# A two-layer transformer, a chunked attention with an RWKV recurrence and a mixture of experts on one core: spreading column values with matmuls instead of transposes

## The reference

```python
def rms_norm(x, g):                       # over the whole token, over one head of 64, or over 128 values
    y = x * lax.rsqrt(jnp.mean(x * x, axis=-1, keepdims=True) + EPS)
    return y * g
...
qa = apply_rope(rms_norm(qa.reshape(bsz, length, H_A, D_A), g_qa), cos, sin)
ka = apply_rope(rms_norm(ka, g_ka), cos, sin)                       # one key head
qb = apply_rope(rms_norm(qb.reshape(bsz, length, H_B, 2, D_B), g_qb), cos, sin)
kb = apply_rope(rms_norm(kb.reshape(bsz, length, H_B, 2, D_B), g_kb), cos, sin)
...
o_b = rms_norm(o_b, g_subln) * (1.0 - lam_init)                     # the attention's sub-norm
...
kk = kk * lax.rsqrt(jnp.maximum(jnp.sum(kk * kk, axis=-1, keepdims=True), 1e-24))   # per head of 64
...
yn = ((y - m) * lax.rsqrt(var + GN_EPS)).reshape(B, S, D_RWKV)      # group norm, per head of 64
```

## Time and profile before

| | |
|---|---|
| median of 3 runs | 2809.46 us (2809.1 to 2816.86) |
| the profiled execution | 2809.1 us, its span 2807.6 us |
| mean granted PE clock | 0.979 |
| PE busy | 2642.6 us, 94% of the span, 14834 records |
| DVE busy | 1647.5 us, 59% |
| ACT busy | 1189.3 us, 42% |
| POOL busy | 138.7 us, 5% |

### The profile page before, as it was taken

The page is one execution under the profiler, slowest core; times in us unless marked ns, Lnnn a source line. Parts: engine busy times, 40 slices in busy tenths (PEclk is TensorE's granted clock), DMA queues, the critical chain, the costliest instruction groups (busy, mean ns, idle before and its releaser), DMA issues.

```text
span 2807.6 us, 36515 instructions
## 1 busy us (share of the span) xinstructions
PE 2642.6 (94%) x14834; PEld 1992.0 (71%) x14834; DVE 1647.5 (59%) x2744; ACT 1189.3 (42%) x1815; POOL 138.7 (5%) x101
## 2 busy tenths in 40 slices
PE   6999999999999999999999999999999989989878
PEld 4777677888876786767888887676776758745446
DVE  4698556645446488655645455445435534489767
ACT  3226543423334224653424234345322324388765
POOL 0020000000000020000000000000000000033210
PEclk9999999999999999999999999999999989999999
DMA  3112232232221222233223222312111124599982
GB/s 139 61 64 102 72 124 98 90 104 91 92 89 64 77 74 81 85 109 109 90 90 105 90 91 90 120 55 78 58 49 42 35 95 142 205 382 396 401 335 97
DMA packets 64144, 334.95 MB, mean 119 GB/s; under 512 B 9570, under 2 KB 10338, under 8 KB 31076
## 3 DMA queue, kind: packets, MB, share of 16 engines
q1 hardware_dynamic: 58852, 324.15, 32.0%
q0 software_dynamic: 5120, 8.40, 0.9%
HBM read 312.59 MB, written 28.31 MB: 121 GB/s over the span
## 4 chain that ended last, share of the span: by engine, by line
PE 84%; DVE 7%; ACT 5%; issue 3%; DMA 1%; SPq 0%; POOLq 0%; DVEq 0%; ACTq 0%
PE bank L911 15%; PE bank L913 15%; PE bank L912 15%; PE bank L1091 4%; PE bank L1093 3%; PE bank L1092 3%; PE bank L3212 2%; PE bank L3213 2%; PE bank L3228 2%; PE bank L2310 2%; PE bank L1135 2%; PE bank L1165 1%; PE bank L1155 1%; PE bank L1082 1%; PE bank L2297 1%
## 5 line engine op out<-in xcount | busy, mean ns | idle before, releaser
L911 PE MATMUL bank<-XH,wh 128*128 128x512 f32 x1328 | 530.5, 399 | 13.2 <-DVE XL L1387 8.9
L913 PE MATMUL bank<-XH,wl 128*128 128x512 f32 x1328 | 519.6, 391 | 0.0
L912 PE MATMUL bank<-XL,wh 128*128 128x512 f32 x1328 | 519.5, 391 | 0.0
L1346 DVE TENSOR_TENSOR wl<-raw,wh 128x2048 fp32r<-128x2048 f32 (+1 forms) x165 | 364.0, 2208 | 155.6 <-ACT wh L1878 155.6
L1878 ACT ACTIVATE wh<-raw 128x2048 fp32r<-128x2048 f32 (+1 forms) x165 | 303.4, 1840 | 178.7 <-DMA raw<-in_W 178.6
L911 PEld LDWEIGHTS bank<-XH,wh 128*128 128x128 f32 x1328 | 249.8, 188 | 87.9 <-DVE XL L1387 18.2
L912 PEld LDWEIGHTS bank<-XL,wh 128*128 128x128 f32 x1328 | 250.3, 188 | 53.4 <-issue 3.2
L913 PEld LDWEIGHTS bank<-XH,wl 128*128 128x128 f32 x1328 | 249.9, 188 | 53.9
L911 PE MATMUL bank<-arena_rounded,wh 128*128 128x512 f32 x576 | 230.6, 400 | 5.3 <-DVE arena_rounded L1592 3.2
L912 PE MATMUL bank<-arena_rounded,wh 128*128 128x512 f32 x576 | 229.1, 398 | 0.0
L913 PE MATMUL bank<-arena_rounded,wl 128*128 128x512 f32 x576 | 229.0, 398 | 0.0
(11 more groups left out here) (541 smaller groups left out, 4478.8 us busy)
## 6 DMA issues: line engine op xcount, KB each, us to landing
raw<-in_W SPq DMA_DIRECT2D x153, 1024.0 KB, 4.9
arena<-in_WE SPq DMA_DIRECT2D x40, 1024.0 KB, 25.6
wh_full<-in_WE SPq DMA_DIRECT2D x19, 1024.0 KB, 26.9
raw<-in_WE SPq DMA_DIRECT2D x18, 1024.0 KB, 26.4
gsave<-scr SPq DMA_DIRECT2D x48, 256.0 KB, 2.2
scr<-gsave SPq DMA_DIRECT2D x48, 256.0 KB, 3.8
hT<-in_WE SPq DMA_DIRECT2D x12, 1024.0 KB, 26.3
cst<-in_WE SPq DMA_DIRECT2D x7, 1024.0 KB, 26.9
```

The costliest lines, as they stand in the source:

```text
L911: pe.matmul(ps[0:c.stop - c.start, :], h[:, k, c], hi, start=i == 0, stop=False)
L912: pe.matmul(ps[0:c.stop - c.start, :], h[:, k, c], lo, start=False, stop=False)
L913: mm = pe.matmul(ps[0:c.stop - c.start, :], l[:, k, c], hi, start=False, stop=i == len(xs) - 1)
L1346: w_lo.inc(dve.tensor_tensor(wl[:, i % 3, 0:k], raw[:, i % 3, 0:k], wh[:, i % 3, 0:k].bitcast(F32), ALU.subtract), i)
```

## The change

Three edits. `spread` calls a matmul with the identity as the moving operand in place of the transpose, on the same operands. `spread_heads` takes the eight columns themselves and makes two matmuls per 128 tokens, each with a column broadcast to 128x64 as its weights and 64 partitions of the bank as its result; the vector engine's writing out of the columns (for `kkspread` and `gspread`) is dropped. For the keys of RoPE the columns of a whole group are transposed once (`hrt`, at steps 5 and 13, in bank 5, 2 or 8 result rows), the scalar engine copies them to SBUF, and each key pair's factor is one matmul of the constants `hbr` (2 or 8 rows, 128 columns) with these rows. The scalar engine's five copies a layer and their semaphore go.

```diff
@@ plan_win
+                if s in (5, 13):
+                    bank.plan(("hrt", li, s // 4 - 1), 5)
@@ spread
-                    mm = pe.transpose(ps[:, tt(ti)], cols[:, ti:ti + 1].to_broadcast([128, 128]), ident)
+                    mm = pe.matmul(ps[:, tt(ti)], cols[:, ti:ti + 1].to_broadcast([128, 128]), ident, start=True, stop=True)
@@ spread_heads(key, cols, ready, warm=0)
-                    mm = pe.transpose(ps[:, tt(ti)], rows[:, tt(ti)], ident)
+                    for h in range(2):
+                        mm = pe.matmul(ps[64 * h:64 * h + 64, tt(ti)], cols[:, ti, h:h + 1].to_broadcast([128, 64]), ident,
+                                       start=True, stop=True)
@@ tensor engine, first_projections
+                    if s in (5, 13):
+                        gi = s // 4 - 1
+                        n = 2 if gi == 0 else 8
+                        ps = opened(("hrt", li, gi))
+                        pe.wait_ge(*hrec((li, gi)))
+                        for ti in range(4):
+                            mm = pe.transpose(ps[0:n, tt(ti)], rr(li, gi)[:, 8 * ti:8 * ti + n], ident)
+                        bank.filled(mm, ("hrt", li, gi))
...
-                            spread_heads(("hbr", li, t), RT[t % 2], factor((li, t)))
+                            gi, j = t // 4, 0 if t == 3 else t % 4
+                            n = 2 if gi == 0 else 8
+                            ps = opened(("hbr", li, t))
+                            pe.wait_ge(*bank.empty(("hrt", li, gi)))
+                            if t == 3 and li == 0:
+                                pe.wait_ge(c_in, 16)
+                            a, _ = cparts["hbr"]
+                            mm = pe.matmul(ps, cst[0:n, a + 128 * j:a + 128 * j + 128], RT[gi % 2][0:n, :], start=True, stop=True)
+                            bank.filled(mm, ("hbr", li, t))
@@ scalar engine, first_projections (behind the square of the step's pair, ahead of the second relu)
-                    t = rope_at(s)
-                    if t is not None and is_key(t):
-                        gi, j = t // 4, 0 if t == 3 else t % 4
-                        act.wait_ge(*hrec((li, gi)))
-                        if t >= 10:
-                            act.wait_ge(*bank.full(("hbr", li, t - 2)))
-                        cols = rr(li, gi).rearrange("p (t h) -> p t h", t=4)[:, :, 2 * j:2 * j + 2]
-                        factor.inc(act.activation(RT[t % 2].rearrange("p (t h d) -> p t h d", t=4, h=2),
-                                                  bc(cols.unsqueeze(3), [128, 4, 2, 64]), ACT.Copy), (li, t))
+                    if s in (5, 13):
+                        gi = s // 4 - 1
+                        n = 2 if gi == 0 else 8
+                        key = ("hrt", li, gi)
+                        act.wait_ge(*bank.full(key))
+                        bank.emptied(act.activation(RT[gi % 2][0:n, :], bank.ap(key)[0:n, :], ACT.Copy), key)
@@ tensor engine, recurrence
-                spread_heads(("kkspread", j), KSQ, pv(("krec", j)), 3 if j else 2)
+                spread_heads(("kkspread", j), p.kcols.rearrange("p (t h) -> p t h", t=4), pv(("krec", j)), 3 if j else 2)
...
-                spread_heads(("gspread", j), GSQ, sv(("grec", j)))
+                spread_heads(("gspread", j), p.gcols.rearrange("p (t h) -> p t h", t=4), sv(("grec", j)))
@@ vector engine, recurrence (the same for gcols, GSQ and grec)
-                v.inc(dve.reciprocal(p.kcols, p.kcols))
-                dve.wait_ge(*v())
-                pv.inc(dve.tensor_copy(KSQ.rearrange("p (x d) -> p x d", x=8), bc(p.kcols.unsqueeze(2), [128, 8, 64])), ("krec", j))
+                pv.inc(dve.reciprocal(p.kcols, p.kcols), ("krec", j))
```

More of the change, by code:

```diff
@@ L588, in program @@
         turned = Signal(sem("turned"), [(li, t) for li in layers for t in range(16) if not is_key(t)])
-        factor = Signal(sem("factor"), [(li, t) for li in layers for t in range(16) if is_key(t)])
         scored = Signal(sem("scored"), [(li, i) for li in layers for i in range(12)])
@@ L957, in spread, with spread_heads @@
                 for ti in range(4):
-                    mm = pe.transpose(ps[:, tt(ti)], cols[:, ti:ti + 1].to_broadcast([128, 128]), ident)
+                    mm = pe.matmul(ps[:, tt(ti)], cols[:, ti:ti + 1].to_broadcast([128, 128]), ident, start=True, stop=True)
                 bank.filled(mm, key)
-            def spread_heads(key, rows, ready, warm=0):
+            def spread_heads(key, cols, ready, warm=0):
                 ps = opened(key)
@@ L2754, in scan @@
                 dve.wait_ge(*sa(("groot", j)))
-                v.inc(dve.reciprocal(p.gcols, p.gcols))
-                dve.wait_ge(*v())
-                sv.inc(dve.tensor_copy(GSQ.rearrange("p (x d) -> p x d", x=8), bc(p.gcols.unsqueeze(2), [128, 8, 64])), ("grec", j))
+                sv.inc(dve.reciprocal(p.gcols, p.gcols), ("grec", j))
                 yield
```

## The result

The changed kernel took 2830.15 us (median of 4 runs, 2827.71 to 2834.76), the kernel before 2811.28 (4 runs). The ratio is 1.0073, 95% interval 1.0052 to 1.0092: slower by 15 to 26 us, 20.5 by the ratio. The prediction was 2812, with a range to 2822. The record has nine executions of the changed kernel: eight lie between 2827.65 and 2837.99 (their mean is 1.0072 times that of the kernel before, the two medians stand at 1.0067), and the ninth, at a mean granted clock of 0.69, took 3555.43 and is left out.

The account below looks back on a forecast made before the run. The prediction took the PE as the bound (busy 94% of the span, 84% of the chain). Terms 4.1 + 1.8 + 3.9 + 0.2 = +10.0 us and -7 for the clock, on 2809.1, gave 2812, range 2800 to 2822.

Parts of the forecast that it names:

- The price of a burst: Spreads as f32 matmuls: +0.45 us on the PE per burst, +0.9 for the first norm at half clock.
- the overlap of the two halves: Head spreads' 16 records on alternating partition halves run concurrently, 1.09 us; without overlap 1.76.
- the copy of 0.6 on two partitions: RoPE's keys: each new small ACT copy of 512 columns takes 0.6 us.
- step 5: RoPE's keys: the new ACT copy ahead of the second relu delays the next scores, +1.38 us a layer.
- step 6: RoPE's keys: without the factor's copy the relu and rotation start earlier, -0.52 us a layer.
- the recurrence: kkspread and gspread without the vector engine's copy: earlier start offsets longer PE bursts, +0.2 us in all.
- steps 13 to 16: RoPE's keys: PE gains 2.1 us, partly absorbed by the idle of 3.07; attention starts +1.1 us later a layer.
- The clock: Low-clock stretches behind PE idles, 16 us at stake, would partly go: -7 us.
- three stage ends: Recurrence: low-clock stretches, one of 3.4 us worth 1.7 and two of 10.2 worth some 3.7 each.
- the low stretches only move: Rival, whole kernel: the terms stand and the clock gives nothing, 2819 us; chance 0.22.
- the sub-norm's first bursts are free: Attention's sub-norm: first two bursts of each layer covered by four waits of 6.7 us; uncovered 1.8.
- The third possibility of the prediction: Rival: the 1.2 us idle at step 5 brings a low-clock stretch in each layer, 2822 us; chance 0.08.

Follow-up runs that it names:

- b_heads: Kernel before with only the recurrence's two head spreads (kkspread, gspread) as matmuls, without the vector engine's copy: 2812.12 us, 1.0012.
- e_twice: Kernel before with every one-column spread's four transposes made twice, no matmul in it: 2821.9 us, 1.0043.
- f_factor: Kernel before with the scalar engine's factor copy of step 6 moved behind the second relu: 2811.36 us, 1.0009.
- n_norms: Kernel before with the one-column spreads as matmuls in the norms alone, the sub-norm's left as transposes: 2819.43 us, 1.0033.
- s_subs: Kernel before with the one-column spreads as matmuls in the sub-norm alone: 2815.99 us, 1.0021.
- a_spread: Kernel before with only the one-column spreads (norms and sub-norm) as matmuls: 2821.65 us, 1.0042.
- c_keys: Kernel before with only RoPE's key factors made the new way: 2821.49 us, 1.0037.
- d_keys_late: c_keys with the scalar engine's new copy behind the second relu of the step: 2821.77 us, 1.0055 to the kernel before.
- r_subs: s_subs profiled once more with nothing edited: span 2832.8 us.

## Why the prediction was wrong, step by step

**Right.** The price of a burst (some 0.45 on the PE, 0.97 for the first norm, 1.09 for the head spread), the overlap of the two halves, the copy of 0.6 on two partitions, step 5 (1.2 measured, 1.38 forecast), step 6 (0.52), and the recurrence, as far as it can be told: `b_heads` costs nothing that stands clear of its interval. The first two mechanisms of steps 13 to 16 came as described: the vector engine's wait for GpSimd grew from 0.46 to 0.73, with two new waits of 0.34 and 0.30 in front of it, 0.91 together where 0.8 was forecast.

**Mis-sized: steps 13 to 16.** The term was +1.1 a layer; the timeline shows 2.5. Of the difference of 1.4, 0.96 is the vector engine's addition beside GpSimd's second product. The prediction followed GpSimd as something that the vector engine waits for, and not as something that slows it. With it, the keys are 1.2 - 0.5 + 2.5 = 3.2 a layer, 6.4 in place of 3.9, and the sum of the rows is 12.5 in place of 10.0.

**Failed: "The clock", -7.** This is the step that put the result outside. Its reason was that low stretches follow waits, that some of these shrink, and that the spreads among these waits are denser as matmuls. Some waits did shrink, as said above, but the stretches did not go with them: their sum rose from 122 to 142 us in the first pair of profiles and fell from 135 to 130 in the second, and behind the cut of 1696.73 it rose in both, from 91 to 105 and from 91 to 103. Measured +20.5 less 12.5 leaves about +8 (2 to 13 by the interval), of the same size as the term and of the other sign. The prediction also counted three stage ends in its 16 us at stake, where the kernel before has four: one of 3.4 us and three of 10.2, the last at 2308.4. Two pairs of profiles tell where it stands. A cut of the vector engine just ahead of the second model's first projection starts at 1696.73 and 1698.72 in the two profiles of before, and at 1713.84 and 1709.33 in the two of after: the second pair is 10.6 apart, which is about the sum of the rows up to there (6.4 for the keys, 1.8 for the sub-norm, 0.96 + 4 x 0.46 for five norms: 11.0). The first pair is 17.1 apart. The early stretches scatter: ahead of the cut there are 31 and 44 us of low clock in the two profiles of before, 38 and 27 in those of after, so the agreement of the second pair with the sum is in part chance. Behind that point the spans grow by another 9.5 and 7.4, where rows explain 1.4 (three norms). So in these pairs 6.0 to 8.1 us are the late stretches', of which the 12 to 14 us more of low clock account for some 4 to 5 by the slopes above: 1.6 at the entry of the second model and 2.6 of the 3.1 at the first stage end, which the second stage end about gives back (3.4 us of low clock where before had 10.2); the rest lies in others that were not taken apart. The mean granted clock shows less of it than the places do: it was 0.9752 over the changed kernel's four runs and 0.9774 over 65 of the kernel before, worth some 3 us by the last point of this document.

The prediction had put "the low stretches only move" among its rivals at 0.22, with a price of nothing. What it missed is that moving has a price. In the kernel before, some of them lie where the PE is not the limit (the vector engine 3.31 of 3.41 us busy at 195.5, 6.47 of 6.82 at 1062.5, 3.40 of 3.40 at 1714.5). A stretch that leaves such a place gives back little. The first of these shows it: `e_twice`, `b_heads`, `f_factor` and `n_norms` have no low stretch there, yet their vector engine takes the same 50.77 us to the first softmax, and the PE, 1.36 us early, waits for it; its second scores start 0.45 behind the softmax where they started 0.55 behind it. The prediction had taken the full 1.7 us of this stretch as gain. One that lands where the others wait for the PE costs 1.6.

**Still open.** Why the stretch at the first stage end is 3.4 us in some kernels, 10.2 or 13.7 in others and missing in `s_subs` wasn't settled; the unedited part behind the cut shows what they cost, not what sets them. For `a_spread` and `n_norms`, which edit three norms there, that the surplus is the clock's is argued and not shown: from the cut to the end they take 1116.7 and 1119.2 us, with 98 and 107 of low clock, but the mean clock of `a_spread` over its six executions (0.9775) is that of the kernel before. Nor is it shown that the sub-norm's first bursts are free: the four waits of 6.7 us that should have shrunk by 1.8 are 6.2 in `s_subs`, but also 5.3 in `n_norms`, which left the sub-norm alone. The third possibility of the prediction, a low stretch brought about by the wait at step 5, is half supported: every profile with the new step 5 has one that starts between 80 and 93 us, no other has, and most of these lack the one at 107 (`c_keys` has both). It came even in `d_keys_late`, where the wait is gone, so it isn't the wait that brings it.

## What to carry to other kernels

When the PE carries 84% of the chain and the granted clock drops in places, cost an edit by its rows, and treat the clock as a term that can go against you by as much as it can help: here 7 us were counted as its gain and some 8 us were lost, more than most of the edits cost. Keep a part of the program that the edit leaves alone and compare it between profiles: what it gains or loses is not the edit's own work. Look at which engine is full in each low stretch before counting on its removal: one in which the others wait for another engine was worth next to nothing here. Where a second engine shares work with the vector engine, follow what starts beside what, and not only what waits for what.

## What the hardware showed that was not expected

- A shift of the PE's stream by 1 to 2 us changed durations elsewhere: the vector engine's addition of 128x512 took 1.65 in place of 0.69, and a product of 128x384 1.70 in place of 0.56, each beside a GpSimd product that started with or just before it.
- The PE can stay at the lower clock while it is full. In `s_subs` and again in `r_subs` the stretch at the third stage end lasted 44.4 us, with the PE busy for 42.5 of them; in the kernel before the clock rose after 10.2 us in the same place, and the PE did 274 records where `s_subs` did 164. Busy by stretch, first `s_subs`, then the kernel before:

```profile
2248.60:2293.00 44.40, 42.55 (x164) 26.02 (x164) 11.37 (x19) 8.71 (x18) 0.00 (x0) 0.50 0.11 36
```

```profile
2250.40:2294.80 44.40, 42.70 (x274) 26.72 (x274) 15.32 (x26) 13.18 (x26) 0.00 (x0) 0.89 0.21 70
```

- On the whole a microsecond at the lower clock cost far less than half a microsecond: over 161 executions of 13 kernels the span grew by 1.5 us (a line fitted to all, with a level for each kernel) for each 0.001 of mean granted clock, which is 5.6 us of low clock: 0.27 for each. In the unedited part of the table it was 0.39.
